# Keys-first mixer, 16 KB weight pieces, paired attention outputs and forget rows, norm squares added on VectorE: one fp32 network in one kernel

## What is computed

```python
# first block (256 tokens x, and 256 context tokens ctx that feed the mixer's states)
mod = silu(c) @ w_mod + b_mod                       # six vectors of 1024
u = modulate(rmsnorm(x), mod);  uc = modulate(rmsnorm(ctx), mod_c)
q, k, v, z = (u @ w_in)                             # 8 heads of 128, q k v: 5-tap conv, silu
q, k = l2norm(q), l2norm(k);    g, beta = gates(u @ w_ab)
o = chunk_gated_delta(q, k, v, g, beta)             # per head and direction: chunks of 64,
                                                    # triangular solve, state carried by a scan
h = x + mod * ((rmsnorm(o) * silu(z)) @ w_out)
aff = softmax(um @ w_router)                        # um = modulate(rmsnorm(h))
h = h + mod * experts(top 32 tokens of each of 16)  # silu(x w_gate) * (x w_up) @ w_down, 2048 wide
h = rmsnorm(h)
# second block, two layers
for l in range(2):
    h = h + 0.5 * swiglu_ffn(rms_norm(h))           # 2816 wide
    z = rms_norm(h) @ w_in                          # lru_x, lru_g, q, k, v, f, gates
    y_lru = (gelu(z_lg) * rg_lru(conv(z_lx))) @ w_lru_out
    s = q @ k.T * scale + cum[i] - cum[j]           # 16 heads of 64, causal, cum = cumsum(logsigmoid(f))
    y_attn = (softmax(s) @ v) @ w_attn_out
    h = h + (g_lru * y_lru + g_attn * y_attn) @ w_o
    h = h + 0.5 * swiglu_ffn(rms_norm(h))
```

## Time and profile before

| | before |
|---|---|
| median of 3 runs | 3033.22 us (3030.31 to 3039.67) |
| the profiled execution | 3037.34 us |
| its span, first to last instruction | 3035.5 us |
| mean granted TensorE clock | 0.915 |
| TensorE busy | 2567.6 us (85%) |
| VectorE, ScalarE, GpSimd busy | 573.3, 428.8, 151.2 us |
| DMA moved | 686.4 MB, mean 226 GB/s |

### The profile page before, as it was taken

The page is one execution under the profiler, slowest core; times in us unless marked ns, Lnnn a source line. Parts: engine busy times, 40 slices in busy tenths (PEclk is TensorE's granted clock), DMA queues, the critical chain, the costliest instruction groups (busy, mean ns, idle before and its releaser), DMA issues.

```text
span 3035.5 us, 34203 instructions
## 1 busy us (share of the span) xinstructions
PE 2567.6 (85%) x15291; PEld 1835.0 (60%) x15291; DVE 573.3 (19%) x1323; ACT 428.8 (14%) x885; POOL 151.2 (5%) x274
## 2 busy tenths in 40 slices
PE   7978877556555555567999999999999999999999
PEld 4756753212111211114888677888888886788888
DVE  2645532000000000001101433110010034231010
ACT  3434311000000000001000234010010012430000
POOL 0354320000000000000000000000000000000000
PEclk9989979777878877777999999999999999999999
DMA  7533339999999999999434343343443443334430
GB/s 264 149 87 107 120 129 404 415 416 418 418 416 417 418 418 416 417 418 380 159 118 153 125 154 123 134 145 128 156 166 126 137 148 125 139 117 160 139 132 35
DMA packets 250239, 686.44 MB, mean 226 GB/s; under 512 B 36684, under 2 KB 73965, under 8 KB 216301
## 3 DMA queue, kind: packets, MB, share of 16 engines
q1 hardware_dynamic: 245741, 683.74, 59.8%
q10 hardware_dynamic: 4352, 0.53, 0.1%
HBM read 680.04 MB, written 4.19 MB: 225 GB/s over the span
## 4 chain that ended last, share of the span: by engine, by line
PE 64%; DMA 27%; POOL 2%; DVE 2%; SPq 2%; ACT 1%; issue 1%; DVEq 0%; ACTq 0%
PE bank L1673 22%; PE bank L1698 10%; PE bank L1799 8%; DMA slab_ring<-in_moe_w_gate 8%; DMA slab_ring_more<-in_moe_w_gate 7%; DMA slab_ring<-in_moe_w_down 5%; DMA slab_ring_more<-in_moe_w_down 5%; PE bank L387 3%; PE bank L1658 3%; PE bank L1722 3%; PE bank L1323 2%; DMA slab_ring<-in_moe_w_up 2%; PE bank L1742 2%; SPq L1237 1%; POOL slab_ring L1105 1%; POOL slab_ring L1103 1%
## 5 line engine op out<-in xcount | busy, mean ns | idle before, releaser
L1673 PE MATMUL bank<-layer_uT,slab_ring 128*128 128x256 f32 x2560 | 553.2, 379 | 0.0
L1673 PEld LDWEIGHTS bank<-layer_uT,slab_ring 128*128 128x128 f32 x2560 | 486.4, 190 | 66.1
L1323 PE MATMUL bank<-slab_ring,chosen_xT 128*32 128x512 f32 x1248 | 208.5, 806 | 134.5 <-DMA slab_ring<-in_moe_w_up 68.8
L1698 PE MATMUL bank<-ffn_hidden,slab_ring 128*128 128x256 f32 x1408 | 304.5, 379 | 0.0
L1698 PEld LDWEIGHTS bank<-ffn_hidden,slab_ring 128*128 128x128 f32 x1408 | 267.5, 190 | 36.4
L1799 PE MATMUL bank<-layer_uT,slab_ring 128*128 128x256 f32 x1024 | 233.7, 382 | 0.0
L1323 PEld LDWEIGHTS bank<-slab_ring,chosen_xT 128*32 128x32 f32 x1248 | 39.7, 129 | 288.6 <-DMA slab_ring<-in_moe_w_up 114.0
L1323 PE MATMUL bank<-slab_ring_more,chosen_xT 128*32 128x512 f32 x800 | 128.4, 773 | 95.9 <-DMA slab_ring_more<-in_moe_w_up 52.6
L1799 PEld LDWEIGHTS bank<-layer_uT,slab_ring 128*128 128x128 f32 x1024 | 189.9, 190 | 31.2 <-issue 7.7
L1323 PE MATMUL bank<-slab_ring,beaten_then_hidden 128*32 128x256 f32 x1216 | 97.0, 479 | 56.7 <-DMA slab_ring<-in_moe_w_down 50.5
L1323 PEld LDWEIGHTS bank<-slab_ring_more,chosen_xT 128*32 128x32 f32 x800 | 24.4, 126 | 196.4 <-DMA slab_ring_more<-in_moe_w_up 83.2
(11 more groups left out here) (375 smaller groups left out, 2535.6 us busy)
## 6 DMA issues: line engine op xcount, KB each, us to landing
slab_ring<-in_w_up SPq DMA_DIRECT2D x44, 2048.0 KB, 7.9
slab_ring<-in_moe_w_up SPq DMA_DIRECT2D x39, 2048.0 KB, 29.4
slab_ring<-in_moe_w_gate SPq DMA_DIRECT2D x39, 2048.0 KB, 26.6
slab_ring<-in_moe_w_down SPq DMA_DIRECT2D x38, 2048.0 KB, 28.8
slab_ring<-in_w_in SPq DMA_DIRECT2D x28, 2048.0 KB, 7.9
slab_ring_more<-in_moe_w_down SPq DMA_DIRECT2D x26, 2048.0 KB, 31.7
slab_ring_more<-in_moe_w_gate SPq DMA_DIRECT2D x25, 2048.0 KB, 27.6
slab_ring_more<-in_moe_w_up SPq DMA_DIRECT2D x25, 2048.0 KB, 28.2
```

Of the source, the lines that this page charges most:

```text
L1323: ins = nc.tensor.matmul(out[32 * c:32 * c + 32, 0:cols], x, slot_of((q * EXPERT_SLABS + i) % NRE).rearrange("p (k n) -> p k n", k=2 if co ...
L1673: i = nc.tensor.matmul(bank[:, (j % 2) * T:(j % 2 + 1) * T], w[:, k * 512 + j * P:k * 512 + (j + 1) * P], x[:, k, :], start=(j % 2 == 0 an ...
L1698: i = nc.tensor.matmul(ps[4 + m // 2][:, (m % 2) * T:(m % 2 + 1) * T], w[:, (k - k0) * D + m * P:(k - k0) * D + (m + 1) * P], hid[:, k, :] ...
```

## The change

Four parts.

1. **Mixer.** TensorE projects q first, then k, then does what stood between (the values of the head before, or the outputs of a pair), then the decay rows of the same head, z, key transposes, square sums, the products of the same head, and v last. q and z have semaphores of their own. The query products go into another bank (4), the modulation's transpose moves to `v_tokens`. ScalarE and VectorE follow: decays, blocks and products come in the head itself, ahead of its v taps (for head 1 behind its v). SP loads q, k, z, v in this order, issues `blocks_in` of a pair ahead of the v weights of the next even head, and the last one ahead of `w_out`.
2. **Experts.** `expert_slab` gives each partition one run of 16 KB: two adjacent rows of gate and up, four adjacent rows of down. The channels of a slab are thus those 2p, 2p + 1 (or 4p to 4p + 3), so the chosen tokens are read with stride 2, the hidden values are transposed with stride 4, and gain and shift of the norm are brought into the new order by eight small matmuls.
3. **Dense layers.** In five of six norms VectorE adds the eight squared pieces to two (three adds), and two matmuls sum them; the first norm keeps eight. The forget rows are also written to partitions 64 to 79, and each head of a pair uses its own copy. The transposed probabilities get two tiles, and both heads' outputs are multiplied in one place (`heads_out`), alternating between the two column halves of the array.
4. **SBUF.** The router's weights and the second probabilities tile share one tile, `router_then_probs`.

The core of the diff:

```diff
         def head_weights(h):
-            for j in (1, 0, 3, 2):
+            for j in (0, 1, 3, 2):
+                if j == 2 and h > 0 and h % 2 == 0:
+                    blocks_in(h // 2 - 1)
...
+        def z_projected(h):
+
+            pe.wait_ge(s_w[3], 16 * (h + 1))
+            got("qconv", h)
...
         def v_tokens(h):
 
+            got("mod_row", h)
+            nc.tensor.transpose(ps[7][:, 0:P], mrow[:], ident)
             got("vsilu", h)
             if h:
-                got("bv", h - 1)
+                got("att", h)
...
-        def head(h, before_tail=None):
+        def head(h, between):
+            q_projected(h)
+            if h == 1:
+                mod_late(0)
             k_projected(h)
-            if before_tail is not None:
-                tail(before_tail)
-            qz_projected(h)
-            v_projected(h)
-            k_tokens(h)
-            square_sums(h)
+            between()
+            if h == 1:
...
+            else:
+                decay_rows(h)
+                z_projected(h)
+                k_tokens(h)
+                square_sums(h)
+                products(h)
+                v_projected(h)
             mod_late(h)
...
-                k_projected(h)
-                outputs(p)
-                qz_projected(h)
-                v_projected(h)
-                k_tokens(h)
-                square_sums(h)
-                mod_late(h)
-                head(h + 1, h)
+                head(h, lambda: outputs(p))
+                head(h + 1, lambda: v_tokens(h))
...
 def expert_slab(env, e, i):
 
     kind, j = GATE_UP_DOWN[i]
     w = env.inputs[{"g": "moe_w_gate", "u": "moe_w_up", "d": "moe_w_down"}[kind]][0]
-    w = w[bass.ds(e, 1)].rearrange("o (k p) n -> p (o k) n", p=P)
-    return w[:, j * 4:j * 4 + 4, :] if kind == "d" else w[:, j * 2:j * 2 + 2, :]
+    return w[bass.ds(e, 1)].rearrange("o (j p r) n -> p (o j) r n", p=P, r=4 if kind == "d" else 2)[:, j]
...
             def norm(n):
+                if l or n:
+                    for half in range(2):
+                        dve.wait_ge(ly.sem["nsq"], ly.value(l, "nsq", 4 * n + 2 * half + 2))
+                        i = nc.vector.tensor_tensor(sqn[:, 4 * half:4 * half + 2, :], sqn[:, 4 * half:4 * half + 2, :], sqn[:, 4 * half + 2:4 * half + 4, :], ALU.add)
+                    i.then_inc(ly.next("nred"), 1)
+                    dve.wait_ge(ly.sem["nred"], ly.value(l, "nred", 2 * n + 1))
+                    nc.vector.tensor_tensor(sqn[:, 0:2, :], sqn[:, 0:2, :], sqn[:, 4:6, :], ALU.add).then_inc(ly.next("nred"), 1)
...
                     for hh in range(2):
-                        row = ident[0:AH, 2 * p + hh:2 * p + hh + 1].to_broadcast((AH, P))
-                        i = nc.tensor.matmul(ps[4 + hh][:, lo:hi], row, fg[:, 2, 0:hi - lo], start=False, stop=True, skip_group_check=True)
+                        r0 = hh * HD
+                        row = ident[r0:r0 + AH, r0 + 2 * p + hh:r0 + 2 * p + hh + 1].to_broadcast((AH, P))
+                        i = nc.tensor.matmul(ps[4 + hh][:, lo:hi], row, fg[r0:r0 + AH, 2, 0:hi - lo], start=False, stop=True, skip_group_check=True)
...
-            def head_out(p, hh):
+            def heads_out(p):
...
+                for t in range(NT):
+                    for hh in range(2):
+                        h, r0 = 2 * p + hh, hh * HD
+                        ob = ps[7][r0:r0 + HD, (p % 2) * T:(p % 2 + 1) * T]
+                        i = nc.tensor.matmul(ob[:, t * P:], vtok[:, t, h * HD:(h + 1) * HD], pT[hh][:, t * T:t * P + T], start=(t == 0), stop=(t == NT - 1), skip_group_check=True)
+                i.then_inc(ly.next("o_ps"), 1)
...
                     elif step and j == 2:
-                        head_out(step - 1, 0)
                         probs_transposed(step - 1, 1)
                     elif step and j == 3:
-                        head_out(step - 1, 1)
+                        heads_out(step - 1)
```

329 lines of the change are left out of this document (176 added, 153 removed).

## The result

| | before | changed |
|---|---|---|
| median | 3034.7 us (the three runs of before and one more, 3030.31 to 3039.67) | 2964.5 us (4 runs, 2963.26 to 2965.53) |
| the profiled execution, its span | 3037.34 us, 3035.5 us | 2965.53 us, 2963.7 us |
| first matmul behind the mixer (the last pair's output projection, L1262 and now L1296) | 438.05 | 425.61 |
| first matmul of the dense layers | 1417.04 | 1382.43 |

What follows compares the result with a forecast made beforehand. Bounds: a chain of waits through all engines in the mixer, DMA for the experts, TensorE in the dense layers. Savings of 24.2 + 23.5 + 13.0 + 10.2 + 11.7, less 1, make 81.6 us: 2952 us, range 2938 to 2978.

Steps and rivals of the forecast that it cites:

- a fixed cost per piece: Experts' stream: 0.62 ns per piece plus 9.42 per 4 KB, so 16 KB pieces run at 428 GB/s, saving 23.5 us.
- The rival of the bank pitch: Experts' stream: partitions 16 KB apart could meet in one memory bank, making the kernel slower, 3083 us; chance 0.04.
- norms: Dense layers: five of six norms lose 6 of 8 sum matmuls, 2.6 us each, 13.0 us saved.
- forget rows: Dense attention: both heads' forget rows run together from different array rows, 0.64 us saved 16 times, 10.2 us.
- outputs: Dense attention: two heads' outputs run side by side in column halves, 0.73 us saved 16 times, 11.7 us.
- The rival drawn from the Trainium skill: Dense attention: the column halves of the two output heads don't run together, 2964 us; chance 0.12.
- A of pair 0: Mixer, first pair: VectorE's last A block, wanted for the inverses, comes at 104.3, 9.5 us earlier than 113.8.
- Levels(0): Mixer, first pair: levels start at 161.5 instead of 171.0, the way from A unchanged, TensorE there at about 160.
- Scan to outputs: Mixer, first pair: q and k stand there, 27.2 us instead of 24.8, so outputs(0) comes 7.1 us earlier.
- The round: Mixer, outputs(0) to outputs(1): 85.0 us instead of 87.1, 2.1 less.
- Last pair: Mixer: levels(3) at 98.0 us after outputs(1) instead of 112.95, 15.0 saved, TensorE and the inverses arriving together.
- A new wait takes the mixer's gain: Mixer: k taps behind q's, bv before the query products, or late weights take half of 24 us, 2964; chance 0.13.

Runs made afterwards that it cites:

- e5: The changed kernel with the experts' pieces as before (8 KB for gate and up, 4 KB for down): 2987.04 us, 22.5 more.
- e6: The changed kernel with down slabs in two 8 KB pieces per partition, gate and up in one of 16 KB: 2967.79 us, 3.3 more.
- e2: The changed kernel with TensorE's gate-sums wait behind head 1's q and k, and head 0's value rows ahead of head 1's k taps: 2956.5 us, 8.0 less.
- e3: e1 with the value transposes of a pair's last head behind its levels' 32-wide products, VectorE's value rows behind its copies: 2952.69 us, 7.9 less than e1.
- e1: The changed kernel with ScalarE's eight loads of pair 0's inverses issued ahead of head 3's value silu, not behind: 2960.62 us, 3.9 less.
- e8: The changed kernel with the two w_out loads held until pair 2's levels reach their 64-wide step: 2964.1 us, no difference that can be told.

## Why the prediction was right and where it was wrong

**Experts: right.** 22.2 us where 22.5 were forecast, by the mechanism named: a fixed cost per piece, 428 GB/s forecast and 427 found. e5 and e6 put 5.09 and 4.97 beside the 4.90 of 16 KB: halving the number of pieces from 512 to 256 saved 0.12, and from 256 to 128 another 0.07, as a fixed cost per piece has it. The rival of the bank pitch has nothing for it: the new layout runs faster than any before.

**Dense layers: right.** By the rows: norms (3.45 - 0.87) x 5 = 12.9 (forecast 13.0), forget rows (1.51 - 0.86) x 16 = 10.4, with 1.51 taken from start to start (10.2), outputs (1.58 - 0.80) x 16 = 12.5 (11.7). That is 35.8 of 37.2; 1.4 us I didn't place. Undone one by one, the last two gave back 10.3 and 11.4 us. The norms' 12.9 stand on their rows alone; no run undid them. The rival drawn from the Trainium skill, "TensorE: Matmul & The Clock Gate", Part 3, The mechanism (weight loads overlap running matmuls only in other row groups), had given 2964 by no gain in the outputs. The rows contradict its use here: the two heads share all rows and start 0.01 us apart. The same page, in Why this matters for your kernels, says that matmuls whose outputs lie in different column groups run concurrently; the trace agrees, and that was the sentence to go by. The time of 2964 came out by accident: two rivals name it, and the outputs' term, by which one of them came to it, was there in full.

**Mixer: wrong by half, 12.4 instead of 24.2.** Step by step, by the ends of the outputs:
- *A of pair 0* came at 106.89, not at 104.3: 2.6 short. The prediction let "the wait for the gates" go. The one of the kernel before (2.30 us, for the gate rates, ahead of the gate sums) did go, but TensorE then waited for the gate sums ahead of q of head 1, which the late modulation's matmuls (3.4 us there) had covered before. That cost 1.96 us and, through the clock, 1.7 more. V of head 1 ended at 95.9 instead of 93.8, and from there A took 11.0 instead of 10.5. e2 took the wait away.
- *Levels(0)*: by A and the 57.2 us of the way they should have let scan(0) start at 175.9 (106.89 + 57.2 + the 11.8 that levels take); it started at 181.66, 5.8 short. ScalarE's loads end last there, at 173.39. Had they not been waited for, scan(0) would start at about 176.6 (an estimate: 166.76 + 1.08 + 0.50, and the 8.27 from 173.39 to the scan), so some 5.1 of it is theirs. The other 0.7 is TensorE, which did not get to the levels "at about 160" but at 166.76, behind a wait of 2.91 for the modulation row and the value transposes; e3 moved these. This is the step that failed: "The way there ... doesn't change. What changes is when A is ready." The way has ScalarE's queue in it, and the change puts a silu ahead of it that waits for VectorE. I had followed SP's queue and not this one. Nor does the sum know that these loads, once late, come behind SP's 512 KB loads and take 5.0 us to land instead of 2.2. e1 took 3.9 us off the total time.
- *Scan to outputs*: 26.8 against 26.0 (23.6 before and the 2.4 that the prediction adds), 0.8 short. Outputs(0) thus end 2.05 us later than before (208.46 against 206.41), where 7.1 earlier was forecast.
- *The round* from outputs(0) to outputs(1): 84.7 against 85.0. Right.
- *Last pair*: 101.8 us from the end of outputs(1) to levels(3) against 97.6, 4.2 short. 2.45 of it is the gap inside levels(2), where TensorE, if the times are read as in e8, waits for instructions; the rest I didn't place. As forecast, TensorE and the inverses have changed places as the bound: levels(3) wait for nothing.
- *Behind levels(3)* 1.3 us less than before, which the sum doesn't have.

Together -9.2 (the first three), +0.3, -4.2, +1.3: 24.2 becomes 12.4. With mixers that end up to 3 us apart from trace to trace, the steps of about 1 us among these are no more than that scatter, and the whole could be read as anything from 10 to 13. The prediction's own signs say the same: levels(0) near 161 and levels(3) near 382 came at 166.76 and 394.92, and the mixer's end near 414 at 425.61. Of the rivals, the one that came true is "A new wait takes the mixer's gain", at 0.13 and with half of the 24 us; but of the three causes that it names, only the wait for bv was there (2.79; the sum has 0.7 for it and the gates' wait together), and the wait that decided was a fourth.

**The total.** In the profiled execution 9.8 us were missing (2965.5 against 2955.7): 11.8 in the mixer, 0.3 in the experts' stage, less 2.3 in the dense layers, whose surplus thus hid a part of the mixer's shortfall. The other 2.7 of the 12.5 between 2952 and 2964.5 are the step from a profiled execution to a median: 4.1 us before, 1.0 now.

## What to carry to other kernels

When work is moved to the end of a block, list everything that stands behind it on its engine, DMA issues included: a queue of loads on a compute engine is as late as the last wait ahead of it. Where one of two engines issues half of a set of transfers, follow both halves, and look what is issued just ahead of the later one: loads of 32 KB landed in 2.2 us before and in 5.0 behind three of 512 KB. A stream that is bound by DMA gains from longer contiguous pieces even beyond 8 KB (here 1.4% from 8 to 16 KB), and small matmuls gain from being given different rows or different columns of the array, whichever they don't fill.
